# The first MLP product of a hybrid encoder block as seven block products, with the residual normalized ahead of it

## The chip, the cores and the metric

One core of one Trainium2 chip runs the whole block in one launch. The metric is device microseconds of that core; a kernel's number is the median of three runs. TensorE (PE) multiplies, VectorE (DVE), ScalarE (ACT) and GpSimd (POOL) do the elementwise work, and the queues of SyncE (SP), ACT and POOL issue the DMAs.

## The reference, cut to what matters

A prompt of 512 tokens and a sample of 256 tokens pass through one layer with shared weights; 16 meta tokens stand ahead of each. All is float32.

```python
u = _rms(h, norm_mix[l])
proj = u @ w_in[l]                      # latents, rotary key, GLU input, gate logits
...                                     # attention and convolution branches
h = h + (g_a * attn + g_c * conv) @ w_out[l]
u = _rms(h, norm_mlp[l])                                             # mean square over 1024 columns
h = h + jnp.square(jax.nn.relu(u @ w_mlp_in[l])) @ w_mlp_out[l]      # 1024 x 4096, then 4096 x 1024
return _rms(h, norm_final)[:, N_META:]
```

The meta tokens are dropped at the end, so from `w_out` on only 768 tokens are computed.

## The kernel before, in words

Every product of two float32 operands is three matmuls of a rounded part and its remainder: hi*hi, hi*lo and lo*hi. A unit is 512 KB of weights. SP loads it into one of four slots of `raw`; ACT rounds it to `whi` (`hi_unit`, L371); POOL subtracts (`lo_unit`, L376) to get `wlo`; PE multiplies (`products`, L389). Each engine has its own program in order, and counters (semaphores) tie them. The stages follow each other on PE: x is normalized and transposed; latents (units 0 to 7); 16 convolution units; 16 gate units; attention over four pairs of heads; `w_o_attn`, `w_conv_out`, `w_out`; first MLP product; second MLP product.

Start: SP issues the meta tokens, three tiles of x, one weight unit, then (after POOL has cleared `tapsrows`) eight small vector loads and the convolution taps, then the other three tiles of x. ACT squares and roots each tile (`x_rms`, L614), DVE scales it (L994), PE transposes it (L1568). PE transposes the taps (L1581) between the third and the fourth tile.

First MLP product: 32 units, each 128 hidden columns over all 1024 inputs, 48 matmuls (half of 512 tokens and half of 256). The residual h is transposed unnormalized (`h_transpose`, 8 times six transposes); the token scale is spread over partitions with 12 matmuls (`spread_rms`, L1885) and multiplied in on DVE while a unit leaves PSUM (L1380); ACT squares (L943). Beside these units 32 copies on SP and 32 accumulating DMAs on POOL (`sum_copy`, `sum_add`, L1468) write sums of two blocks of `w_mlp_out` to DRAM.

Second MLP product: seven products of block sums in place of eight (`MIX`), 8 units each. For one product the sum is not in DRAM: ACT negates the loaded block in place (L914) and a POOL DMA adds the other block to it (L1555). ACT rounds, DVE subtracts (L1366), hidden blocks are combined and split (L1360, L929, L1370).

## Time and profile before

| what | us |
|---|---|
| median of 3 runs (1288.31 to 1291.43) | 1289.13 |
| profiled execution | 1290.69 |
| its span, first to last instruction | 1289.1 |
| PE busy / DVE / ACT / POOL | 1251.3 / 738.5 / 490.5 / 394.8 |
| mean granted clock of PE | 0.994 |

The profiled execution is 1.6 us longer than its span; what is counted in the trace is the span. PE busy is the union of its matmuls; what a matmul costs is read from the spacing of starts, since their modelled ends overlap.

### The profile page before, as it was taken

How to read it: one execution, taken by the hardware profiler on the slowest of the kernel's cores; microseconds unless marked ns; L12 is line 12 of the kernel's file. 1: busy time of each engine (PE TensorE's matmuls, PEld its weight loads, DVE VectorE, ACT ScalarE, POOL GpSimd, SP SyncE). 2: the span in 40 equal slices, each digit the busy share in tenths (PEclk: the TensorE clock that was granted, in tenths of full speed). 3: DMA queues.
4: the chain of work that ended last, by engine and by line, in shares of the span. 5: the costliest groups of instructions: out<-in, count | busy, mean ns of one | idle time of the engine just before them, and what ended most of it. 6: DMA issues, size and time to landing. Idle time of an engine off the chain costs nothing.

```text
span 1289.1 us, 18449 instructions
## 1 busy us (share of the span) xinstructions
PE 1251.3 (97%) x7037; PEld 1083.4 (84%) x7037; DVE 738.5 (57%) x888; ACT 490.5 (38%) x737; POOL 394.8 (31%) x252
## 2 busy tenths in 40 slices
PE   5999999999999999989999999999999999999997
PEld 4888888888888998878888888888888888887886
DVE  4205999999977877784743123111011136876887
ACT  5234211122256666663522134211222234455455
POOL 1443322233333333326322323344444310020101
PEclk8999999999999999999999999999999999999999
DMA  6222212333220101104344135777777664386443
GB/s 186 69 71 53 76 51 66 90 115 108 87 74 17 35 22 29 49 1 149 109 122 177 66 131 131 181 188 189 187 186 193 137 190 131 131 199 183 125 131 114
DMA packets 145926, 146.55 MB, mean 114 GB/s; under 512 B 11231, under 2 KB 107549, under 8 KB 145868
## 3 DMA queue, kind: packets, MB, share of 16 engines
q1 hardware_dynamic: 132684, 118.48, 29.8%
q0 software_dynamic: 10880, 20.97, 9.4%
q10 hardware_dynamic: 2304, 6.29, 1.2%
q8 instruction: 39, 0.64, 0.2%
q14 instruction: 19, 0.16, 0.0%
HBM read 136.29 MB, written 42.99 MB: 139 GB/s over the span
## 4 chain that ended last, share of the span: by engine, by line
PE 86%; issue 4%; DVE 4%; ACT 2%; POOL 2%; DMA 1%; SPq 0%; POOLq 0%; ACTq 0%; DVEq 0%
PE psum L389 55%; PE psum L1918 17%; PE psum L1839 5%; PE psum L1715 3%; PE psum L1745 2%; POOL wlo L376 1%; PE psum L1680 1%; PE psum L1603 1%; PE psum L1727 1%; DMA xt<-in_x_prompt 1%; DVE ptlo L1166 1%; DVE negmax L1154 1%; DVE olo L1231 1%; PE psum L1846 0%; ACT uhi L623 0%
## 5 line engine op out<-in xcount | busy, mean ns | idle before, releaser
L376 POOL TENSOR_TENSOR wlo<-raw,whi 128x1024 fp32r<-128x1024 f32 (+1 forms) x112 | 258.5, 2308 | 511.4 <-ACT whi L371 511.2
L1074 DVE SCALAR_TENSOR_TENSOR psum<-cs,convw,psum 128x799 f32<-128x799 f32 x196 | 189.4, 1048 | 0.0
L371 ACT ACTIVATE whi<-raw 128x1024 fp32r<-128x1024 f32 (+1 forms) x112 | 112.8, 1007 | 123.4 <-PE psum L389 76.0
L1380 DVE SCALAR_TENSOR_TENSOR hid<-psum,rbc 128x768 f32 (+1 forms) x32 | 30.6, 958 | 218.1 <-PE psum L389 218.0
L389 PE MATMUL psum<-uhi,whi 128*128 128x512 f32 x592 | 152.3, 338 | 0.8 <-POOL wlo L376 0.8
L389 PE MATMUL psum<-uhi,wlo 128*128 128x512 f32 x592 | 152.9, 339 | 0.0
L389 PE MATMUL psum<-ulo,whi 128*128 128x512 f32 x592 | 152.6, 339 | 0.0
L389 PE MATMUL psum<-u2hi,whi 128*128 128x512 f32 (+1 forms) x512 | 130.8, 336 | 0.0
L389 PE MATMUL psum<-u2lo,whi 128*128 128x512 f32 (+1 forms) x512 | 130.3, 335 | 0.0
L389 PE MATMUL psum<-u2hi,wlo 128*128 128x512 f32 (+1 forms) x512 | 130.3, 335 | 0.0
L943 ACT ACTIVATE hid<-hid (+1 forms) x32 | 27.1, 847 | 202.3 <-DVE hid L1380 202.3
L389 PEld LDWEIGHTS psum<-uhi,whi 128*128 128x128 f32 x592 | 91.4, 188 | 14.8 <-POOL wlo L376 1.6
L389 PEld LDWEIGHTS psum<-uhi,wlo 128*128 128x128 f32 x592 | 91.7, 188 | 12.9
L389 PEld LDWEIGHTS psum<-ulo,whi 128*128 128x128 f32 x592 | 91.5, 188 | 12.4
L1918 PE MATMUL psum<-whi,hidhi 128*128 128x512 f32 x228 | 88.9, 390 | 1.2 <-DVE hidlo L1370 1.2
L1918 PE MATMUL psum<-whi,hidlo 128*128 128x512 f32 x228 | 88.7, 389 | 0.0
L1918 PE MATMUL psum<-wlo,hidhi 128*128 128x512 f32 x228 | 88.7, 389 | 0.0
L389 PEld LDWEIGHTS psum<-u2lo,whi 128*128 128x128 f32 x512 | 77.7, 188 | 11.2
L389 PEld LDWEIGHTS psum<-u2hi,wlo 128*128 128x128 f32 x512 | 77.6, 188 | 11.1
L389 PEld LDWEIGHTS psum<-u2hi,whi 128*128 128x128 f32 x512 | 77.6, 188 | 11.0
L1366 DVE TENSOR_TENSOR wlo<-raw,whi 128x1024 fp32r<-128x1024 f32 x38 | 46.5, 1224 | 34.6 <-ACT whi L923 34.6
L923 ACT ACTIVATE whi<-raw 128x1024 fp32r<-128x1024 f32 x38 | 40.2, 1058 | 61.4 <-PE psum L1918 58.0
(243 smaller groups left out, 2455.4 us busy)
## 6 DMA issues: line engine op xcount, KB each, us to landing
raw<-in_w_in SPq DMA_DIRECT2D x38, 512.0 KB, 4.0
raw<-in_w_mlp_in SPq DMA_DIRECT2D x32, 512.0 KB, 4.1
wsums<-in_w_mlp_out SPq DMA_DIRECT2D x32, 512.0 KB, 7.2
wsums<-in_w_mlp_out POOLq DMA_DIRECT2D x32, 512.0 KB, 7.4
raw<-wsums SPq DMA_DIRECT2D x32, 512.0 KB, 3.3
raw<-in_w_mlp_out SPq DMA_DIRECT2D x24, 512.0 KB, 3.7
gates<-gout ACTq DMA_DIRECT2D x16, 384.0 KB, 2.3
gin<-gates SPq DMA_DIRECT2D x16, 384.0 KB, 3.1
```

Of the source, the lines that this page charges most:

```text
L371: nc.scalar.activation(whi[:, c % 2, 0:w], raw[:, c % 4, 0:w], ACT.Copy).then_inc(hi_ready, 1)
L376: gp.tensor_tensor(out=wlo[:, c % 2, 0:w], in0=raw[:, c % 4, 0:w], in1=whi[:, c % 2, 0:w].bitcast(F32), op=ALU.subtract).then_inc(lo_ready, 1)
L389: mm = nc.tensor.matmul(out[:, o0:o0 + n], a, b[:, k, c0:c0 + n], start=first and step == 0, stop=last and step == 2)
L923: nc.scalar.activation(whf[m % 3], raw[:, m % 4], ACT.Copy).then_inc(wmhi_ready, 1)
L943: nc.scalar.activation(r, r, ACT.Square).then_inc(hid_ready, 1)
L1074: ins = nc.vector.scalar_tensor_tensor(out=out, in0=src, scalar=w, in1=a, op0=ALU.mult, op1=ALU.add)
L1366: nc.vector.tensor_tensor(out=wlf[m % 3], in0=raw[:, m % 4], in1=whf[m % 3].bitcast(F32), op=ALU.subtract).then_inc(wmlo_ready, 1)
L1380: nc.vector.scalar_tensor_tensor(out=hid[:, ds(i * 4 + c, 1), :], in0=psum[:, pair:pair + 1, 0:TQ], scalar=0.0, in1=rbc[:, :].rearrange("p ...
L1715: mm = nc.tensor.matmul(psum[:, q % 2, e * HALF:e * HALF + n], a[:, c0:c0 + P], b[:, grp["k0"] + k0:grp["k0"] + k0 + n], start=step == 0, ...
L1745: mm = nc.tensor.matmul(bank[:, 7, 0:2 * P], a[:, vt, hh * VD:(hh + 1) * VD], r[:, blk % 2, e, :], start=e == 0 and step == 0, stop=False)
L1839: mm = nc.tensor.matmul(out, a, b[:, kk, :], start=first and step == 0, stop=last and step == 2)
L1918: mm = nc.tensor.matmul(bank[:, FF_BANKS[p % 2][tt]], a, b[:, kk, :], start=jj == 0 and kk == 0 and step == 0, stop=jj == STEPS - 1 and kk ...
```

## The change

1. The first MLP product is done as seven products of blocks (`IN_MIX`): hidden columns in two halves, tokens in two thirds of 384 each (prompt and sample together are 768), inputs in two halves of 512. A unit is 512 inputs by 256 hidden columns, 24 matmuls of 384 columns; there are 56 units. Blocks of `hid` are first copied from PSUM on ACT with their sign, later contributions are added or subtracted on DVE (`hid_drain`), and after the last one DVE does relu and square in one instruction.
2. The residual is scaled by its token's rms before it is transposed (`h1n`, `h_scale`), so `diag`, `rbc` and `spread_rms` go. 16 groups of three transposes are evicted to `u2raw`; sums of its blocks are made by DVE (`u2_sum`), rounded by ACT and subtracted by DVE.
3. The right half of `w_out` is taken in another order: tiles 0 to 2 of units 2 and 3, tiles 3 to 5 of unit 2, the first four transpose groups, tiles 3 to 5 of unit 3.
4. The sums of `w_mlp_in` blocks (`isums`, 32 copies and 32 accumulating DMAs) are made beside convolution and gates, those of `w_mlp_out` beside attention; nothing of that is left beside the MLP. One product of the first MLP product, like one of the second, is negated on ACT and added by a POOL DMA; in the first MLP product POOL also does the subtractions, in program order with those DMAs.
5. The weights of both MLP products use a ring of six slots (`mraw`, remainder written over the raw block). `MIX` is reordered so that its first product needs blocks finished before the last first-stage product.
6. x is loaded first, five tiles ahead of the first weight unit; the small vectors go by ACT's queue; taps are loaded after three more weight units and transposed after unit 2.

```diff
-SUMS = (((0, 0), (1, 0)), ((1, 0), (1, 1)), ((0, 1), (1, 1)), ((0, 0), (0, 1)))
+SUMS = (((0, 1), (1, 1)), ((0, 0), (1, 0)), ((1, 0), (1, 1)), ((0, 0), (0, 1)))
+IN_SUMS = (((1, 0), (1, 1)), ((0, 0), (0, 1)), ((0, 1), (1, 1)), ((1, 0), (0, 0)))
+IN_MIX = (
+    dict(a=((1, 0), (1, 1)), b=((0, 0),), to=((1, 0, 1), (1, 1, -1))),
+    dict(a=((1, 1),), b=((1, 0), (0, 0)), sign=-1, to=((1, 0, 1), (0, 0, -1))),
+    dict(a=((0, 0), (0, 1)), b=((1, 1),), to=((0, 0, -1), (0, 1, 1))),
+    dict(a=((0, 0),), b=((0, 1), (1, 1)), sign=-1, to=((0, 1, 1), (1, 1, -1))),
+    dict(a=((1, 1), (0, 0)), negate=True, b=((0, 0), (1, 1)), sign=1, to=((0, 0, 1), (1, 1, -1))),
+    dict(a=((0, 1), (1, 1)), b=((1, 0), (1, 1)), sign=1, to=((0, 0, 1),)),
+    dict(a=((1, 0), (0, 0)), b=((0, 0), (0, 1)), sign=1, to=((1, 1, 1),)),
+)
...
 # SP
-            for i in X_ORDER[:4]:
+            for i in X_ORDER[:5]:
                 load_x(i)
             columns(win, 0, 0, 0, slice(0, P))
...
             def conv_units(i):
                 for c in range(4):
...
+                    in_sum_copy(c, i)
...
+                for h in range(2):
+                    for c in range(4):
+                        sum_copy(c, i * 2 + h)
...
+            for x in range(2 * IN_UNITS):
+                if x < 4:
+                    sp.wait_ge(lo_ready, U_OUT + 5 + x)
                 else:
-                    sp.wait_ge(wmlo_ready, m - 3)
+                    sp.wait_ge(unit_used, U_IN + x - RING + 1)
...
+                sp.dma_start(x_place(x), x_block(x, 0)).then_inc(m_landed[x % RING], 16)
 # ACT
+            for name, (r, n) in VEC.items():
+                act.dma_start(vecrows[r:r + n, :], t[name][0].rearrange("(k p) -> k p", p=P)).then_inc(consts_landed, 16)
             act.wait_ge(setup, 5)
...
+            for m in range(IN_UNITS):
+                p, jj = m // STEPS, m % STEPS
+                if m + 2 < IN_UNITS:
+                    x_hi(m + 2)
+                else:
+                    mix_hi(m + 2 - IN_UNITS)
+                for n, (_, _, sign) in enumerate(IN_MIX[p]["to"]):
+                    if in_visits(p, n)[0] == p:
...
+                        nc.scalar.activation(c_block(m, n), c_banks(m), ACT.Copy, scale=float(sign)).then_inc(hid_copied, 1)
+                x_negate(m + 4)
+                if p + 1 < len(IN_MIX) and jj in (3, 4):
+                    u2_hi(p + 1, jj - 3)
 # DVE
+            for m in range(IN_UNITS):
...
+                hid_drain(m)
+                if p + 1 < len(IN_MIX):
+                    if jj in (4, 5):
+                        u2_lo(p + 1, jj - 4)
+                    if jj in (2, 3):
+                        u2_sum(p + 1, jj - 2)
+                if m == IN_UNITS - 4:
+                    mix_hidden(0)
+                if m in (IN_UNITS - 3, IN_UNITS - 2):
+                    mix_lo(m - IN_UNITS + 3)
 # POOL
             def conv_step(i):
                 for c in range(4):
                     lo_unit(gp, U_CONV, i, c + 1)
+                    in_sum_add(c, i)
...
                         gp.tensor_scalar(prob[:, q % 2, 0:n], prob[:, q % 2, 0:n], rsum[:, q % 4:q % 4 + 1], 1.0,
                                          ALU.mult, ALU.mult).then_inc(p_ready, 1)
+                        if 1 <= q < 5:
+                            sum_add(q - 1, p * 2 + hh)
...
+            def x_add(x):
+                if x_negated(x):
+                    gp.wait_ge(wneg_ready, negated_before(x + 1))
+                    gp.dma_start(x_place(x), x_block(x, 1), accum_op=ALU.add).then_inc(wsum_landed[x % 3], 16)
+            for x in range(IN_UNITS):
+                gp.wait_ge(mhi_ready, x + 1)
+                gp.tensor_tensor(out=mlo[x % RING], in0=mraw[x % RING], in1=mhi[x % 3].bitcast(F32),
+                                 op=ALU.subtract).then_inc(inlo_ready, 1)
+                if x + 2 < IN_UNITS:
+                    x_add(x + 2)
 # PE
+            for c in range(2):
+                right_half(c, range(NT), c == 0).then_inc(unit_used, 1)
+            right_half(2, range(TT), False)
+            right_half(3, range(TT), True)
+            right_half(2, range(TT, NT), False).then_inc(unit_used, 1)
+            for n in range(4):
...
+                h_transposes(n)
+            right_half(3, range(TT, NT), True).then_inc(unit_used, 1)
+            for m in range(IN_UNITS):
...
+                pe.wait_ge(inlo_ready, m + 1)
...
+                    wait(pe, hid_copied, in_copies(m - 1))
+                    wait(pe, hid_added, in_adds(m - 1))
...
+                for k in range(KD // 2):
...
+                    if 1 <= m < 4:
+                        h_transposes(4 * m + k)
+                    uh, ul = u2hi[p % 2][:, k, :], u2lo[p % 2][:, k, :]
+                    for e in range(2):
+                        for step, (a, b) in enumerate(((wh, uh), (wh, ul), (wl, uh))):
+                            mm = nc.tensor.matmul(bank[:, 2 * (m % 2) + e, 0:THIRD], a[:, k, e * P:(e + 1) * P], b,
+                                                  start=k == 0 and step == 0, stop=k == KD // 2 - 1 and step == 2)
+                mm.then_inc(unit_used, 1)
```

## Rows read from the trace of the kernel before

**Rows 1.** Windows: length, busy (count) PE, PEld, DVE, ACT, POOL, clock, DMA.
```profile
145.00:368.00 223.00, 223.00 (x1271) 195.66 (x1271) 220.64 (x247) 45.66 (x48) 68.36 (x30) 1.00 0.30 87
368.00:568.00 200.00, 191.05 (x1379) 174.90 (x1378) 148.13 (x242) 132.10 (x286) 73.56 (x78) 1.00 0.11 30
797.00:1051.00 254.00, 254.00 (x1468) 222.13 (x1467) 32.87 (x35) 55.52 (x62) 99.33 (x59) 1.00 0.73 182
1056.00:1281.00 225.00, 224.37 (x987) 185.20 (x988) 176.12 (x192) 112.48 (x142) 19.81 (x14) 1.00 0.51 145
```

**Rows 2.** Chain that ended last; columns: start, duration (us), what ran.
```profile
462.88 1.42 PE psum L1745 x12
795.82 1.34 PE psum L1885 x12
797.15 253.78 PE psum L389 x1464
1050.96 0.97 DVE hid L1380
1056.23 110.46 PE psum L1918 x486
```

**Rows 3.** Timeline of the start: start, duration (us), engine, operation, [idle before].
```profile
3.32 0.63 SPq L483 DMA_DIRECT2D vecrows<-in_norm_mix  x1
5.51 1.06 ACT L614 ACTIVATE junk<-xt 128x1024 f32<-128x1024 f32 x1 [0.94 <-DMA xt<-in_x_prompt]
6.55 0.25 SPq L484 DMA_DIRECT2D tapsrows<-in_conv_w  x1
6.89 1.04 ACT L614 ACTIVATE junk<-xt 128x1024 f32<-128x1024 f32 x1
16.40 1.06 PE L1581 MATMUL psum<-ident,tapsrows 32*128 32x32 f32 x8 [4.53 <-DMA tapsrows<-in_conv_w]
17.63 1.06 ACT L614 ACTIVATE junk<-xt 128x1024 f32<-128x1024 f32 x1 [6.68 <-DMA xt<-in_x_prompt]
20.14 3.25 PE L1568 MATMUL psum<-ident,xt 128*128 128x128 f32 x14 [2.69 <-DVE xt L994]
```

**Rows 4.** Timeline of POOL beside the first MLP product, one unit.
```profile
820.86 2.40 POOL L376 TENSOR_TENSOR wlo<-raw,whi 128x1024 fp32r<-128x1024 f32 x1 [4.91 <-ACT whi L371]
823.21 1.05 POOL L1468 DMA_DIRECT2D wsums<-in_w_mlp_out  x1
```

**Rows 5.** Groups by line, shapes apart: count, busy us, mean ns, idle before.
```profile
L371 ACT ACTIVATE whi<-raw 128x1024 fp32r<-128x1024 f32 x96 | 100.9, 1051 | 122.2 <-PE psum L389 76.0 <-PE psum L1839 37.4 <-ACT gout L707 7.5
L1380 DVE SCALAR_TENSOR_TENSOR hid<-psum,rbc 128x768 f32 x24 | 23.0, 958 | 176.8 <-PE psum L389 176.8
```

**Rows 6.** Accumulating DMAs into SBUF (line 1555): issue to landing, of 8.
```profile
DMA to landing us min/median/max: 6.5/7.3/8.8
```

**Rows 7.** POOL timeline of line 1555, first and last of eight.
```profile
1133.41 1.23 POOL L1555 DMA_DIRECT2D raw<-in_w_mlp_out  x1 [91.75 <-ACT raw L914]
1167.35 1.20 POOL L1555 DMA_DIRECT2D raw<-in_w_mlp_out  x1 [3.64 <-ACT raw L914]
```

**Rows 8.** DMA queues from 1130 to 1180 us: packets, MB, share of 16 engines.
```profile
q0 software_dynamic: 2176, 4.19, 53.6%
q1 hardware_dynamic: 2724, 6.26, 35.5%
```

**Rows 9.** DMA issues of the page: count, KB each, median us to landing.
```profile
raw<-in_w_mlp_in SPq DMA_DIRECT2D x32, 512.0 KB, 4.1
```

**Rows 10.** Timeline of POOL in attention: two neighbouring scalings of the probabilities.
```profile
461.27 0.72 POOL L1503 TENSOR_SCALAR prob<-prob,rsum 128x528 f32<-128x528 f32 x1 [1.27 <-DVE rsum L1160]
462.64 0.49 POOL L1503 TENSOR_SCALAR prob<-prob,rsum 128x272 f32<-128x272 f32 x1 [0.65 <-DVE rsum L1160]
```

**Rows 11.** Timeline of POOL and DVE where two operations overlap.
```profile
96.95 2.40 POOL L376 TENSOR_TENSOR wlo<-raw,whi 128x1024 fp32r<-128x1024 f32 x1
97.08 3.10 DVE L1023 TENSOR_TENSOR krt<-krt,krsw 128x784 f32<-128x784 f32 x1 [1.01 <-POOL krsw L1463]
```

More of the change, by code:

```diff
@@ L422, in sum_squares @@
             mm.then_inc(ss_mm, 1)
[L424 to L432 removed]
+        wm = t["w_mlp_out"][0].rearrange("(u b a p) n -> p u b a n", a=2, b=2, p=P)
@@ L447, in hid_block, with c_banks, u2_block, u2_source @@
+        def c_banks(m):
+            return psum[:, m % 2, :].rearrange("p (b n) -> p b n", b=2)[:, :, 0:THIRD]
+        def u2_block(p, which, part):
+            half, tokens = IN_MIX[p]["b"][which]
+            return u2raw[:, 4 * half + 2 * part:4 * half + 2 * part + 2, tokens * THIRD:(tokens + 1) * THIRD]
+        def u2_source(p, part):
+            if len(IN_MIX[p]["b"]) > 1:
+                return u2sum[p % 2][:, 2 * part:2 * part + 2, :]
+            return u2_block(p, 0, part)
         def hid_block(m, which):
@@ L1351, in _, with h_add @@
-            dve.wait_ge(rbc_mm, 1)
-            nc.vector.tensor_copy(rbc[:, :], psum[:, 2, 0:TQ]).then_inc(rbc_ready, 1)
-            dve.wait_ge(rbc_ready, 1)
+            def h_add(half, i):
+                if half == 0:
+                    tile_made(out_tile, U_OUT + 4, 0, i)
+                elif i < NT - 1:
+                    dve.wait_ge(right_tile, i + 1)
+                else:
+                    dve.wait_ge(unit_used, U_IN)
+                dve.wait_ge(h_landed[0 if i < 4 else 1], 16)
+                hx = h1[:, i, half * HALF:(half + 1) * HALF]
+                nc.vector.tensor_tensor(out=hx, in0=bank[:, (4 + 6 * half + i) % 8], in1=hx, op=ALU.add).then_inc(h_ready, 1)
@@ new lines, in h_scale, with u2_sum @@
+            def h_scale(i):
+                dve.wait_ge(h_root, i + 1)
+                nc.vector.reciprocal(rstd[:, i:i + 1], root[:, i:i + 1]).then_inc(h_rstd, 1)
+                dve.wait_ge(h_rstd, i + 1)
+                dve.wait_ge(h_ready, NT + i + 1)
+                nc.vector.tensor_scalar(h1n[:, i], h1[:, i], rstd[:, i:i + 1], None, ALU.mult).then_inc(h_scaled, 1)
+            def u2_sum(p, part):
+                if len(IN_MIX[p]["b"]) > 1:
+                    dve.wait_ge(u2_act, 4)
+                    dve.wait_ge(u2_dve, 4 if p == 1 else 12)
+                    if p > 1:
+                        dve.wait_ge(unit_used, U_IN + (p - 1) * STEPS)
+                    nc.vector.tensor_tensor(out=u2_source(p, part), in0=u2_block(p, 0, part), in1=u2_block(p, 1, part),
+                                            op=ALU.add if IN_MIX[p]["sign"] > 0 else ALU.subtract).then_inc(usum_ready, 1)
@@ new lines, in u2_lo, with u2_evict @@
+            def u2_lo(p, part):
+                dve.wait_ge(u2hi_ready, 2 * p + part + 1)
+                if p > 1:
+                    dve.wait_ge(unit_used, U_IN + (p - 1) * STEPS)
+                nc.vector.tensor_tensor(out=u2lo[p % 2][:, 2 * part:2 * part + 2, :], in0=u2_source(p, part),
+                                        in1=u2hi[p % 2][:, 2 * part:2 * part + 2, :].bitcast(F32), op=ALU.subtract).then_inc(u2lo_ready, 1)
+            def u2_evict(n):
+                half, k = turned(n)
+                dve.wait_ge(u2t_ready, n + 1)
+                nc.vector.tensor_scalar(u2raw[:, k, half * THIRD:(half + 1) * THIRD], bank[:, turned_bank(n), 0:THIRD],
+                                        vcol("norm_mlp", k), None, ALU.mult).then_inc(u2_dve, 1)
@@ L1900, in _, with right_half @@
-            rolled(pe, KF // 4, in_step, peel=1, last=1)
+            def right_half(c, tiles, by_tile):
+                pe.wait_ge(lo_ready, U_OUT + 4 + c + 1)
+                wh, wl = weights(c % 2, 2, HALF)
+                order = [(kk, tt) for tt in tiles for kk in range(2)] if by_tile else [(kk, tt) for kk in range(2) for tt in tiles]
+                for kk, tt in order:
+                    if c == 0 and kk == 0:
+                        out_bank_free(1, tt)
+                    a_hi, a_lo = z(0, c, kk, tt)
+                    for step, (a, b) in enumerate(((a_hi, wh), (a_hi, wl), (a_lo, wh))):
+                        mm = nc.tensor.matmul(bank[:, (10 + tt) % 8], a, b[:, kk, :], start=c == 0 and kk == 0 and step == 0,
+                                              stop=c == 3 and kk == 1 and step == 2)
+                    if c == 3 and kk == 1 and tt < NT - 1:
+                        mm.then_inc(right_tile, 1)
+                return mm
```

404 lines of the change are left out of this document (210 added, 194 removed).

## The prediction

> **What bounds the kernel now.** I first read busy time by stage. In the convolution and gate stage and beside the first MLP product PE is busy in every microsecond, in the second MLP product for 224.4 of 225, in attention for 191 of 200 [rows 1]: the kernel is a queue of matmuls, and the clock is 1.00 in all four windows. Other engines matter only where they make PE wait. Second I read the chain of waits for what a matmul costs and for the seams: in the first MLP product it stays on PE for 253.78 us and 1464 matmuls, then leaves PE from 1050.96 to 1056.23 us, when the last unit goes through relu, square, rounding and subtraction before the second product can begin [rows 2]. Third the timeline of the start, where PE waits 4.53 us for the taps and 2.69 us for the fourth tile of x [rows 3]. Idle time of DVE, ACT and POOL beside the MLP is what the change spends.
>
> **First MLP product.** Before: 32 units of 48 matmuls, half of 512 and half of 256 columns, 384 on average. The chain gives 253.78/1464 = 0.1734 us per matmul [rows 2], so 8.32 us a unit and 266.3 us in all. After: 56 units of 24 matmuls, all of 384 columns. No row has 384 columns. Below: halfway between 256 columns (1.42/12 = 0.118 us) and 512 (110.46/486 = 0.2273 us) is 0.1728; above: the old mean itself, 0.1734 [rows 2]. I take 0.1734, which is measured on this operand mix: 1344 x 0.1734 = 233.0 us, 4.16 us a unit. **Gain 33.3 us**, at most 34.
>
> **What hides the added work in a unit of 4.16 us.** POOL: a subtraction of 2.40 us [rows 4]. ACT: a rounding of 1.05 us, and at most two copies of 768 elements out of PSUM, which I price like DVE's eviction of the same size, 0.96 us [rows 5]; 3.0 us. DVE: at most two additions and one relu-square of 0.96 us, in some units a block sum or a remainder of the same size, 3.8 us. All fit. A result two units old frees the banks, so a late drain has a whole unit of slack. Weights for a unit are now loaded five units, 21 us, ahead, and landed in 4.1 us before [rows 9]. If that cover goes, each unit costs PE what the longest engine needs over 4.16 us; that happens in one place, below.
>
> **The seams.** The 12 matmuls of `spread_rms` go: 1.34 us [rows 2]. The residual's transposes are 48 before and after. The gap of 1056.23 - 1050.96 = 5.3 us goes [rows 2]: the reordered `MIX` needs blocks finished by the sixth product, and ACT and DVE prepare the first two units during the last three units of the first product. Late next is DVE's third preparation: behind two drains it ends about as PE reaches it; I cost that at nothing, at most 1 us. Ahead of the first unit PE has 18 matmuls of `w_out` (18 x 0.2273 = 4.1 us) while tile 2 is added, squared, rooted and scaled, some 3 us by operations like those of [rows 3, 5]; nothing, at most 1.5 us. **Gain 6.6 us.**
>
> **The start.** The fourth tile of x is squared at 17.63 us because its DMA is issued behind eight vector loads and the taps (3.32 to 6.55 us). Tiles one and two are squared at 5.51 and 6.89, so a fourth that is issued with them comes at 5.51 + 3 x 1.38 = 9.6 [rows 3]. ACT now issues the vector loads itself, 3.2 us of issue at SP's pace; it has a table load and the meta tile to do before 5.51, so I add 1.1 us: 10.7 in place of 17.63, 6.9 us earlier. Upper bound: PE's two waits together, 7.2. The taps' transposes (1.06) leave the start and come back after unit 2, so 1.0 is taken off; lower bound 2, if the fourth tile lands late. **Gain 5.9 us.**
>
> **Sums beside convolution, gates and attention.** POOL issues 32 more DMAs of 1.05 us [rows 4] in the first two stages, where it is busy 68 of 223 us, and the DMA share is 0.30 there; the same sums beside 512 KB loads made 0.73 [rows 1]. The new sums have 1 KB rows in place of 2 KB: the share is between 0.7 and, if a row costs the same whatever its length, just above 1. Loads are issued three units (25 us) ahead, and nothing waits for these sums until the MLP: nothing. SP is moved past 64 copies, each waiting only for the copy before it. In attention POOL's 32 issues stand between scalings of probabilities, for which PE waits. Between the fourth and the fifth scaling POOL is idle 0.65 us [rows 10], less than 1.05, so the fifth comes 0.4 to 0.6 us late; PE has a 1.42 us block ahead of that transpose [rows 2]. I take **1 us lost**, between 0 and 32 x 0.6 = 19.
>
> **The negated product.** Here the change adds a wait. In product 4 ACT negates a block, a POOL DMA adds the other, ACT rounds the sum, POOL subtracts. POOL's program is: subtract x, then issue the addition for x+2. Subtraction x waits for rounding x, which waits for addition x to land. So the addition for x+2, and every subtraction behind it, stands behind the landing for x: a loop of two units of 7.3 us to land [rows 6] + 1.05 to round [rows 5] + 2.40 to subtract [rows 4] + 0.2 between engines = 10.95 us, where PE takes 8.32. Eight units make three full turns: 3 x 2.63 = 7.9 us; the first comes some 0.5 us late, and the added row lengths (1 KB) lengthen the landing a little. I take **9 us lost**. Lower end 4.5: landing 6.5 [rows 6] and 1 us of lead. Upper end 28: landing 8.8, a second issue time of 1.2 [rows 7] and a second engine time, 0.536 x 50/8 = 3.35 us [rows 8], make the loop 17.0, so 3 x 8.7 and a late start. I stay near the median, as the bytes are the same as in that row.
>
> A rule is weighed against this. DVE's sum of two SBUF operands, 784 elements, took 3.10 us and ended 0.8 us after a POOL subtraction that began just before it [rows 11], while DVE's 768 take 0.96 alone [rows 5]. The Trainium skill, "SBUF — State Buffer", its part on the two separate sides of the memory, says that a DVE operation with two SBUF inputs and a GpSimd operation that reads SBUF exclude each other for the whole instruction. The trace agrees in this pair. What it would do here is the first rival below.
>
> **Sum.** 33.3 + 6.6 + 5.9 - 1 - 9 = 35.8 us. From the profiled execution, 1290.69: 1254.9; that execution is 1.6 above the median of the runs, so on their scale 1253.3. I say **1254**, by its own bounds 1243 to 1272.
>
> **Rivals.**
> - *POOL and DVE take turns.* The relu-squares, block sums and remainders have two SBUF operands; with a subtraction they need 2.40 + 2 x 0.96 = 4.3 us of a 4.16 us unit in a few units, which slack takes up, but in product 4 up to three remainders delay subtractions in the loop: 3 x 0.96. **1257**, chance 0.14. For: [rows 11]; against: they collide only if they start so.
> - *The negated product costs nothing.* In the second MLP product the eight additions went out every (1167.35 - 1133.41)/7 = 4.85 us [rows 7], over PE's 4.1 us, and PE was short of work for 0.6 us in the whole stage [rows 1]: lead absorbed it. **1245**, chance 0.17. Against: there no subtraction stood in POOL's queue.
> - *The sums cost where they are made.* The late scalings reach PE each time: 19 us in place of 1. **1272**, chance 0.14. For: attention is the stage where PE already waits 9 of 200 us [rows 1]; against: a block of PE work lies between.
> - *Slower.* In attention four additions are issued within some 8 us. One took 3.35 us of all DMA engines into SBUF [rows 8], so four need 13. Before, they came one in about 8 us or 4.85. If POOL's issue holds the engine until the queue has room, the scalings wait: 5 us and more in each of 8 half pairs. 36/8 = 4.5 us is the point from which the gain is gone; at 6 us, 48 lost: **1302**. Chance 0.05: the issues in the trace took 1.05 and 1.2 us [rows 4, 7], but none came so close together.
> - The remaining 0.02: effects cancel and no change is seen.
>
> **Numbers.** The forecast's own case has 0.48, and with the rivals of 1245 and 1257 it fills 1243 to 1272, which also reaches the third rival's edge. What a measurement of this kernel can tell from no change is about 0.3%, 4 us. Faster 0.93 (the forecast and the first three rivals), same 0.02, slower 0.05.
>
> **What would show it.** First product: 24 matmuls in 4.16 us, starts 0.173 apart. Units 32 to 39: PE waiting for POOL's subtraction, in every second unit by some 2.6 us, ACT's rounding waiting for a DMA. No gap between the products. The fourth tile's transposes near 13 us in place of 20.14 [rows 3]. Attention as long as before within 2 us. Wrong, if PE waits outside product 4 by more than 5 us in sum, if the 384-column matmul starts further than 0.18 apart, or if the convolution stage stretches.

## The result, and the profile after

The changed kernel takes **1259.55 us** (median of 4 runs, 1257.99 to 1263.15), the kernel before, run beside it, 1289.14 (4 runs, 1288.31 to 1291.43): ratio 0.9772, 95% interval 0.9747 to 0.9796. The forecast was 1254 with a range of 1243 to 1272. The profiled execution took 1260.22 us for a span of 1258.6, at a mean granted clock of 0.996.

Where the time went is read from starts of matmuls in both timelines. A line is the same matmul in both; the last column is what the stretch since the line above gained.

| first matmul of | before, us | after, us | gained |
|---|---|---|---|
| the fourth pair of convolution units | 144.76 | 141.67 | 3.1 |
| `w_o_attn` | 573.11 | 570.30 | -0.3 |
| first MLP product | 780.36 | 774.28 | 3.3 |
| second MLP product | 1050.76 | 1020.58 | 24.1 |
| (the last matmul) | 1281.45 | 1250.98 | 0.3 |

In the third line 1.3 us is only moved: 24 transposes of the residual stood in that stretch before, and 12 do after; they are now in the first product. So the first product gained 25.4 and the stretch ahead of it 2.0. The seven block products of the first product are counted from 0: product 3 is units 24 to 31, the negated product 4 units 32 to 39.

Windows by stage of the changed kernel, in the columns of [rows 1] (convolution and gates, attention, first product, second product):

```profile
141.00:365.00 224.00, 223.81 (x1275) 195.94 (x1274) 221.63 (x248) 45.98 (x48) 98.47 (x58) 1.00 0.90 207
365.00:566.00 201.00, 191.77 (x1386) 175.71 (x1385) 148.75 (x244) 132.95 (x288) 108.47 (x111) 1.00 0.82 186
776.00:1020.00 244.00, 237.08 (x1369) 234.22 (x1368) 161.01 (x138) 100.44 (x114) 152.14 (x63) 1.00 0.50 138
1021.00:1251.00 230.00, 228.34 (x1007) 188.40 (x1005) 176.36 (x195) 114.38 (x144) 20.66 (x14) 1.00 0.49 144
```

Against [rows 1], PE is as busy in the first two stages as before, although the DMA share there went from 0.30 and 0.11 to 0.90 and 0.82 (the sums) and POOL is busy for 30 and 35 us more. In the first product PE, which never waited, now idles for 6.9 us; DVE went from 33 to 161 us busy.

The chain that ended last, from the first product on (columns of [rows 2]):

```profile
794.23 88.42 PE psum L2095 x510
...
898.91 3.16 DVE u2sum L1474
...
902.09 0.02 ACT u2hi L1024
...
902.84 1.05 ACT whi L1007
...
903.98 3.01 POOL rawlo L1725
906.98 6.19 DMA raw<-in_w_mlp_in
...
947.31 2.39 POOL rawlo L1725
949.75 70.99 PE psum L2095 x408
1020.74 130.62 PE psum L2116 x576
1151.38 8.70 DMA raw<-in_w_mlp_out
```

A matmul of 384 columns takes 88.42/510 = 0.1734 us. The chain leaves PE at 882.65 us already. Up to 902 it runs over DVE's additions, relu-squares and block sums of product 3. The block sum at 898.91 releases a rounding on ACT (902.09); behind that, in ACT's program, stands the rounding of the next weights (902.84), behind that POOL's subtraction and the second addition (906.98). From there to 950 us the chain goes round POOL's subtraction and the landing of an addition: the loop of the negated product. From issue to issue its turns of two units take 9.7, 9.7 and 12.5 us (906.98, 916.69, 926.35, 938.84). The DMA share from 904 to 944 is 1.00, so how much of a landing is queueing for DMA engines stays open. Between the two products the chain stays on PE. It leaves it once more at 1151.38, for an addition in the second product's negated part.

The timeline of PE, only the rows where it waited in the first product (a last one at 949.75 waited 0.97 us for POOL), and then the POOL and DVE timelines at the end of product 3:

```profile
903.93 0.41 PE L2095 MATMUL psum<-u2hi,whx 128*128 128x384 f32 x1 [0.49 <-DVE hid L1509]
...
909.73 0.41 PE L2095 MATMUL psum<-u2hi,whi 128*128 128x384 f32 x1 [1.36 <-DVE hid L1509]
...
914.88 0.41 PE L2095 MATMUL psum<-u2hi,whi 128*128 128x384 f32 x1 [0.72 <-DVE hid L1509]
...
933.03 0.44 PE L2095 MATMUL psum<-u2hi,whx 128*128 128x384 f32 x1 [0.85 <-POOL rawlo L1725]
...
938.93 0.45 PE L2095 MATMUL psum<-u2hi,whi 128*128 128x384 f32 x1 [1.44 <-POOL rawlo L1725]
...
944.31 0.44 PE L2095 MATMUL psum<-u2hi,whi 128*128 128x384 f32 x1 [0.94 <-POOL rawlo L1725]
```

```profile
898.17 3.07 POOL L1725 TENSOR_TENSOR rawlo<-raw,whx 128x1024 fp32r<-128x1024 f32 x1 [3.59 <-ACT whx L1007]
901.18 1.34 POOL L1721 DMA_DIRECT2D raw<-in_w_mlp_in  x1
...
938.84 1.28 POOL L1721 DMA_DIRECT2D raw<-in_w_mlp_in  x1
```

```profile
898.03 0.96 DVE L1515 SCALAR_TENSOR_TENSOR hid<-hid 128x768 f32<-128x768 f32 x1
898.91 3.15 DVE L1474 TENSOR_TENSOR u2sum<-u2raw 128x768 f32<-128x768 f32 x1
901.98 1.81 DVE L1509 TENSOR_TENSOR hid<-hid,psum 128x768 f32<-128x768 f32 x2
```

Two different engines keep PE waiting: DVE in product 3 (the wait at 914.88, ahead of product 4's first unit, is for product 3's last additions), POOL in the last four units of product 4. The eight additions go out (938.84 - 901.18)/7 = 5.38 us apart. DVE's block sum (L1474) takes 3.15 us beside the subtraction that runs from 898.17 to 901.24, and ends 0.8 after its end; on its own, at 895.32, the same line takes 0.94. The addition out of PSUM (L1509, two in 1.81) is not lengthened. Additions land about as [rows 6] led to expect (all sixteen of both products; the eight of the first take 6.1 to 9.0):

```profile
DMA to landing us min/median/max: 6.0/7.5/10.5
```

The timeline of the start, against [rows 3]:

```profile
10.96 1.04 ACT L708 ACTIVATE junk<-xt 128x1024 f32<-128x1024 f32 x1
...
13.45 2.34 POOL L425 TENSOR_TENSOR wlo<-raw,whi 128x1024 fp32r<-128x1024 f32 x1 [9.95 <-ACT whi L420]
...
13.88 0.22 DVE L1123 COPY vec<-psum 128x62 f32<-128x62 f32 x1 [1.84 <-PE psum L1760]
...
14.20 2.13 DVE L1114 TENSOR_SCALAR xt<-xt,rstd 128x1024 f32<-128x1024 f32 x1
...
16.39 2.71 PE L1750 MATMUL psum<-ident,xt 128*128 128x128 f32 x14 [2.56 <-DVE xt L1114]
```

The fourth tile is squared at 10.96 in place of 17.63. But its scaling stands in DVE's program behind the copy of the vectors, and then takes 2.13 us beside a POOL subtraction (the other tiles' took 0.75), so its transposes come at 16.39 in place of 20.14.

### The profile page after: what moved, and what is told of

It reads as the page before. It is cut to its first block, busy times and chain, and to the rows that moved or that the text cites. A ratio compares the mean times of both kernels' runs of the same rounds, so it can differ in the third digit from the quotient of the medians.

```text
span 1258.6 us, 18355 instructions
## 1 busy us (share of the span) xinstructions
PE 1217.3 (97%) x6833; PEld 1081.8 (86%) x6833; DVE 860.9 (68%) x984; ACT 528.9 (42%) x785; POOL 512.6 (41%) x316
## 4 chain that ended last, share of the span: by engine, by line
PE 78%; issue 7%; DMA 4%; POOL 3%; DVE 3%; ACT 3%; SPq 0%; ACTq 0%; POOLq 0%; DVEq 0%
PE psum L438 34%; PE psum L2116 17%; PE psum L2095 14%; PE psum L2024 3%; PE psum L2062 3%; PE psum L1900 2%; DMA raw<-in_w_mlp_in 2%; PE psum L1930 2%; POOL wlo L425 1%; PE psum L1781 1%; DMA wsums<-in_w_mlp_out 1%; POOL rawlo L1725 1%; PE psum L1912 1%; DMA raw<-in_w_mlp_out 1%; PE psum L1750 1%
## 5 line engine op out<-in xcount | busy, mean ns | idle before, releaser
L425 POOL TENSOR_TENSOR wlo<-raw,whi 128x1024 fp32r<-128x1024 f32 (+1 forms) x80 | 181.9, 2274 | 302.6 <-ACT whi L420 299.4
L1509 DVE TENSOR_TENSOR hid<-hid,psum 128x768 f32<-128x768 f32 x64 | 59.4, 949 | 70.8 <-PE psum L2095 38.4
L2095 PE MATMUL psum<-u2hi,whi 128*128 128x384 f32 x296 | 100.0, 338 | 4.5 <-POOL rawlo L1725 2.4
L438 PEld LDWEIGHTS psum<-ulo,whi 128*128 128x128 f32 x592 | 91.5, 188 | 12.5
L2095 PE MATMUL psum<-u2hi,rawlo 128*128 128x384 f32 x304 | 101.7, 335 | 0.0
L2095 PE MATMUL psum<-u2lo,whi 128*128 128x384 f32 x296 | 98.9, 334 | 0.0
L2116 PE MATMUL psum<-rawlo,hidhi 128*128 128x512 f32 x228 | 88.7, 389 | 0.0
L1007 ACT ACTIVATE whx<-raw 128x1024 fp32r<-128x1024 f32 x38 | 40.2, 1058 | 62.7 <-PE psum L2116 27.7
L1725 POOL TENSOR_TENSOR rawlo<-raw,whi 128x1024 fp32r<-128x1024 f32 x19 | 49.6, 2609 | 39.4 <-ACT whi L1007 39.4
L1725 POOL TENSOR_TENSOR rawlo<-raw,whx 128x1024 fp32r<-128x1024 f32 x19 | 50.5, 2660 | 30.9 <-ACT whx L1007 30.9
L1007 ACT ACTIVATE whi<-rawx 128x1024 fp32r<-128x1024 f32 x36 | 38.1, 1057 | 51.3 <-PE psum L2116 25.7
```

The lines of the kernel that those rows point to most:

```text
L425: gp.tensor_tensor(out=wlo[:, c % 2, 0:w], in0=raw[:, c % 4, 0:w], in1=whi[:, c % 2, 0:w].bitcast(F32), op=ALU.subtract).then_inc(lo_ready, 1)
L438: mm = nc.tensor.matmul(out[:, o0:o0 + n], a, b[:, k, c0:c0 + n], start=first and step == 0, stop=last and step == 2)
L1007: nc.scalar.activation(mhi[x % 3], mraw[x % RING], ACT.Copy).then_inc(mhi_ready, 1)
L1509: nc.vector.tensor_tensor(out=block_, in0=block_, in1=c_banks(m), op=ALU.add if sign > 0 else ALU.subtract).then_inc(hid_added, 1)
L1725: gp.tensor_tensor(out=mlo[x % RING], in0=mraw[x % RING], in1=mhi[x % 3].bitcast(F32), op=ALU.subtract).then_inc(inlo_ready, 1)
L2095: mm = nc.tensor.matmul(bank[:, 2 * (m % 2) + e, 0:THIRD], a[:, k, e * P:(e + 1) * P], b, start=k == 0 and step == 0, stop=k == KD // 2 - ...
```

## The experiments

Three theories of the 9.4 us that the first product loses (246.3 us from its first matmul to the second product's, less 233.0 of matmuls and 36 x 0.109 of transposes). **Theory 1**: the loop of product 4 (round, subtract, issue, land) sets it. **Theory 2**: the DMA engines do. **Theory 3**: DVE and POOL take turns. All kernels were timed in 5 rounds against the kernel before. "Product" is the length from the first matmul of the first product to the first of the second, read from each timeline; it leaves out what happens earlier, which scatters by 2 us (last section). It scatters itself: in the five profiles whose edits leave the work of the first product alone (the changed kernel, after_again, scale_first, no_sums, seam_late) it is 245.3 to 247.1, so a difference of less than about 2 us shows nothing. "PE idle" is 70 less PE's busy time from 880 to 950 us.

| kernel | median us (lowest to highest) | ratio, interval | product | PE idle |
|---|---|---|---|---|
| after_again | 1259.78 (1258.88 to 1262.31) | 0.9772 [0.9759, 0.9785] | 246.1 | 6.7 |
| three_ahead | 1261.50 (1253.99 to 1262.50) | 0.9765 [0.9741, 0.9789] | 245.2 | 5.5 |
| late_relu | 1266.03 (1264.64 to 1268.90) | 0.9820 [0.9806, 0.9833] | 251.2 | 4.8 |
| scale_first | 1258.75 (1258.08 to 1262.43) | 0.9764 [0.9751, 0.9777] | 247.1 | 6.9 |
| relu_on_act | 1261.61 (1260.42 to 1262.63) | 0.9780 [0.9767, 0.9793] | 245.7 | 5.2 |
| relu_on_act_three | 1252.02 (1249.95 to 1255.24) | 0.9713 [0.9694, 0.9732] | 240.6 | 2.8 |
| no_addition | 1257.43 (1256.56 to 1258.57) | 0.9749 [0.9735, 0.9762] | 241.9 | 3.8 |
| no_sums | 1260.74 (1258.94 to 1263.71) | 0.9777 [0.9761, 0.9794] | 245.3 | 6.1 |
| zero_remainders | 1258.22 (1256.19 to 1261.59) | 0.9761 [0.9746, 0.9776] | 241.2 | 2.8 |
| seam_late | 1262.76 (1260.77 to 1264.97) | 0.9785 [0.9771, 0.9798] | 245.6 | 6.8 |
| start_alone (edit of before) | 1287.84 (1285.52 to 1289.35) | 0.9980 [0.9971, 0.9989] | | |
| all_four | 1259.38 (1258.67 to 1262.41) | 0.9766 [0.9753, 0.9779] | 238.9 | 1.4 |

**after_again**, the base of the first group, unedited.

> The changed kernel, nothing edited: the base that the other kernels of this group are compared with. All theories: 1259.5 us, within 1.5, and the kernel before at 1289.

As expected.

**three_ahead**, the loop over three units in place of two:

```diff
-                x_negate(m + 4)
+                x_negate(m + 5)
...
-                if x + 2 < IN_UNITS:
-                    x_add(x + 2)
+                if x + 3 < IN_UNITS:
+                    x_add(x + 3)
```

> ACT negates a block one unit earlier (five units ahead in place of four) and POOL issues the addition for unit x+3, not x+2, behind the subtraction of unit x. Theory 1, the loop 'landing, rounding, subtraction, next issue' over two units sets the 5.38 us of a unit in product 4: the loop now spans three units, 10.95/3 = 3.65 us a unit, below PE's 4.16, so PE's four waits for POOL's subtraction (4.2 us by the profile, about 5 with the ends of the matmuls modelled) go: 1254.5 us, and the additions go out about 4.2 us apart. Theory 2, the DMA engines are the limit (3.35 us for an addition and 1.65 for a load make 5.0 us a unit): the additions still go out about 5.0 us apart, landing takes longer than 7.5 us, ACT's wait for it stays: 1258 to 1260 us. Theory 3, POOL and DVE take turns: POOL's waits go in part, the three waits for DVE at the end of product 3 (2.6 us) stay under each theory.

None of the three forecasts came. The two longest of PE's four waits in the product (the others are 0.51 and 0.55, for DVE too), the window in which the clock fell (columns of [rows 1]), and one of the additions on POOL:

```profile
910.90 0.41 PE L2095 MATMUL psum<-u2hi,whi 128*128 128x384 f32 x1 [1.39 <-DVE hid L1509]
...
918.33 0.41 PE L2095 MATMUL psum<-u2hi,whi 128*128 128x384 f32 x1 [3.01 <-DVE hid L1509]
```

```profile
920.00:924.00 4.00, 4.00 (x17) 4.00 (x16) 2.76 (x2) 1.06 (x1) 3.25 (x2) 0.62 0.96 131
```

```profile
931.37 1.29 POOL L1721 DMA_DIRECT2D raw<-in_w_mlp_in  x1 [3.41 <-ACT raw L998]
```

All waits for POOL are gone, as theory 1 says. But the additions came no closer, (934.56 - 897.19)/7 = 5.34 us apart, where theory 1 had 4.2 and theory 2 5.0. Two of them wait on POOL for ACT's negation (2.75 us at 918.27, 3.41 at 931.37), and ACT waited for the plain load under it. That load could go out only when PE had freed its slot: the one behind 931.37 went out at 924.35, after PE's long wait. So this run does not show that the loop alone set the pace before. POOL's work also comes closer together at the end of product 3 (subtractions from 905.15, 908.98 and 912.41), and DVE, which takes turns with it, is later (a remainder at 912.60 takes 3.75): the waits for DVE grew from 2.6 to 5.5 us. After the longest one the granted clock averaged 0.62 over 4 us, that is, part of them at the lower of the clock's two levels (1.00 is 2.4 GHz, 0.50 is 1.2 GHz): 17 matmuls, where the next windows of 4 us, at 1.00, show 25. One of the five runs took 1253.99; no trace shows what it did otherwise.

**late_relu**, product 3's relu-squares moved to product 5:

```diff
-                for n in range(len(IN_MIX[p]["to"])):
-                    if in_visits(p, n)[-1] == p:
-                        block_ = c_block(m, n)
+                done = [c_block(m, n) for n in range(len(IN_MIX[p]["to"])) if in_visits(p, n)[-1] == p and p != 3]
+                if p == 5:
+                    done.append(c_block(m - 2 * STEPS, 0))
+                for block_ in done:
...
```

> The relu-squares of the block finished by product 3 (eight of 768 elements, two SBUF operands) are made in product 5 in place of product 3. Theory 3, DVE is late at the end of product 3 because its operations with two SBUF operands take turns with POOL's subtractions (2.4 to 3.2 us each in place of 0.96), and these waits add to the time: the three waits go, 1256.5 us. Theory 1 or 2, the additions of product 4 free-run from the first issue near 901 us, and PE only arrives earlier in front of them: the three waits for DVE go, the waits for POOL in product 4 grow by as much, 1259.5 us, within 0.7.

PE's timeline, three of its five waits in the product (0.51 and 1.36 for DVE stand ahead of the last):

```profile
922.96 0.69 PE L2097 MATMUL psum<-u2hi,whi 128*128 128x384 f32 x1 [2.50 <-POOL wlo L1727]
...
939.53 0.44 PE L2097 MATMUL psum<-u2hi,whi 128*128 128x384 f32 x1 [2.33 <-POOL rawlo L1727]
...
992.24 0.41 PE L2097 MATMUL psum<-u2hi,whx 128*128 128x384 f32 x1 [2.69 <-DVE hid L1509]
```

Product 3's waits for DVE went. In product 4 the waits for POOL became fewer and longer, 4.8 us in place of the base's 4.4, and the mean granted clock of 908 to 950 us was 0.92 in place of 1.00: PE came earlier to additions that had kept their pace, as theory 1 said, and some of what had been won went in clock. What no theory had: the eight relu-squares now make product 5 late, in the pattern of product 3 (4.6 us for DVE). The kernel is 6 us slower than the base.

**scale_first**, DVE's program at the start:

```diff
-            x_scale(0), x_scale(1), x_scale(2), x_scale(3)
+            x_scale(0), x_scale(1), x_scale(2), x_scale(3), x_scale(4)
             dve.wait_ge(vec_t, 1)
             nc.vector.tensor_copy(vec[:, :], bank[:, 6, 0:NVEC]).then_inc(vec_ready, 1)
-            x_scale(4)
```

> DVE scales the fourth tile of x before it copies the vectors out of PSUM, not behind. Theory A, the fourth tile's scaling (14.20 us, and 2.13 long beside a POOL subtraction) is what PE waits for: the scaling runs near 11.7 for 0.75 us, its transposes directly behind that of the vectors near 13.7 in place of 16.39, first matmul near 16.4 in place of 18.76, and 2.3 us of it last to the end: 1257.2 us. Theory B, something else is late next (the rounding of the first weights at 12.33 and its POOL subtraction to 15.8, or loads of the next units): the first matmul moves by under 1 us, or PE waits later in the first 60 us: above 1258.5 us.

Timeline of the start:

```profile
12.71 0.75 DVE L1114 TENSOR_SCALAR xt<-xt,rstd 128x1024 f32<-128x1024 f32 x1
...
13.91 2.22 PE L1749 MATMUL psum<-ident,xt 128*128 128x128 f32 x14
...
16.18 0.47 PE L1780 MATMUL psum<-uhi,whi 128*128 128x512 f32 x1
```

Theory A in the trace: the scaling takes 0.75 and the first matmul is at 16.18 in place of 18.76. At the first matmul of `w_o_attn` the kernel is still 2.5 us ahead of the base (the two later kernels with this edit, relu_on_act_three and all_four, 1.6 and 1.5). In the time only 1.0 is seen, less than the runs scatter: in this execution the stretch up to the first product took 2.3 us longer and the product, whose work this edit leaves alone, 1.0 longer: PE waited 3.28 us for POOL at 940.11.

**relu_on_act**, product 3's relu-squares by ACT, in no later product:

```diff
+                if 3 * STEPS <= m - 2 < 4 * STEPS:
+                    block_ = c_block(m - 2, 0)
+                    act.wait_ge(hid_added, in_adds(m - 1))
+                    nc.scalar.activation(block_, block_, ACT.Relu).then_inc(hid_relu, 1)
+                    act.wait_ge(hid_relu, m - 1 - 3 * STEPS)
+                    nc.scalar.activation(block_, block_, ACT.Square).then_inc(hid_whole, 1)
```

> The eight relu-squares that end product 3 are made by ACT (a relu and a square of 768 elements, two units after DVE's addition), not by DVE: nothing is moved into a later product. Theory 1, product 4's additions free-run from the first issue near 901 us, 5.3 us apart, so PE that comes earlier only waits longer there: DVE's three waits at the end of product 3 (2.3 to 2.6 us) go, POOL's in product 4 grow by as much, 1259.8 us, within 1. Theory 3, the waits for DVE are a loss of their own: 1257 us. In the kernel with the relu in product 5 both happened and product 5's waits for DVE (4.6 us) came on top; here product 5 has none.

1261.61, and PE waits for DVE nowhere in the product. Three waits for POOL of 2.54, 1.60 and 1.09 us, 5.2 together, stand where the base has 4.4 in five, and the mean clock from 908 to 950 us is 0.96. The product is 0.4 us shorter than the base's, which is within its scatter: theory 1's side, though the time lies 0.8 us above its range.

**relu_on_act_three**, the three edits above together (three_ahead, scale_first, relu_on_act).

> Three edits together: ACT makes product 3's relu-squares, negation and additions run one unit earlier, and the fourth tile of x is scaled before the vectors are copied. If both waits are what is lost in the first product (DVE beside POOL at the end of product 3, and the loop of additions in product 4), and each edit alone only moved the loss to the other, then together PE waits under 2 us in the whole product and its clock stays at 1.00 there: 1251 us, within 2. If DMA throughput sets product 4 (additions 5.3 us apart with every edit so far), PE still waits for POOL at the end of product 4, 3 us or more: 1255 to 1258 us.

**1252.02 us**, the best of all kernels. The window of 908 to 950 us and the waits of PE in the product:

```profile
908.00:950.00 42.00, 39.23 (x225) 38.39 (x224) 27.49 (x22) 22.49 (x25) 30.78 (x16) 1.00 0.84 194
```

```profile
919.42 0.45 PE L2101 MATMUL psum<-u2hi,whi 128*128 128x384 f32 x1 [1.36 <-POOL wlo L1731]
...
933.77 0.41 PE L2101 MATMUL psum<-u2hi,whi 128*128 128x384 f32 x1 [1.41 <-DVE hid L1515]
```

Each edit alone had moved the loss to the other engine; together they remove 5.5 of the 9.4 us. The forecast's 1251, within 2, came, with 2.8 us of waiting in place of under 2. The additions now go out 4.74 us apart (894.02 to 927.17), still over PE's 4.16, and the DMA share is 0.95 to 1.15 in each 4 us from 900 to 936: with the loop widened, full DMA engines (theory 2) are the likely pace, argued from this share and not tested. The first addition goes out earlier (894 in place of 901), and PE waits for POOL only once.

**no_addition**: product 4 reads a plain block (no negation, no addition).

```diff
-    return (IN_MIX[x // STEPS] if x < IN_UNITS else MIX[x // STEPS - len(IN_MIX)]).get("negate", False)
+    return x >= IN_UNITS and MIX[x // STEPS - len(IN_MIX)].get("negate", False)
```

> Left out: the negation and the addition in product 4 of the first MLP product, whose weights are then one plain block (its result is another). This is the upper bound of what the negated product costs. Theory 1: POOL's waits in product 4 (4.4 us) and the part of DVE's at the end of product 3 that the issues of additions bring about go: 1252 to 1254 us, with up to 2.5 us of DVE's waits left, as the subtractions of POOL stay. Theory 3, taking turns alone makes most of the loss: above 1256 us.

1257.43, on theory 3's side: without the loop PE still waits, for DVE, 3.7 us (0.49, 1.36 and 1.83). Leaving the addition out, alone, takes 246.1 - 241.9 = 4.2 us off the product.

**no_sums**: all 64 sums, their copies and the waits for them left out, plain blocks loaded in their place.

```diff
-                    in_sum_copy(c, i)
...
-                        if 1 <= q < 5:
-                            sum_add(q - 1, p * 2 + hh)
...
```

> Left out: all 64 sums of weight blocks beside convolution, gates and attention (copies, additions and the waits on them); the products read a plain block of the weights in place of each sum (rows of 512 bytes or 2 KB in place of whole sums). The forecast had 1 us for them, all in attention: 1259 us, attention shorter by 0.5 to 1. Rival, the sums cost more than the waits show (DMA share 0.9 beside convolution and gates): 1255 us or less, convolution and gates shorter too.

Windows of the two stages, to be held against those of the changed kernel above:

```profile
141.00:365.00 224.00, 223.81 (x1275) 195.88 (x1273) 221.63 (x248) 46.00 (x48) 69.02 (x31) 1.00 0.30 87
365.00:566.00 201.00, 191.85 (x1388) 175.87 (x1387) 148.75 (x244) 133.25 (x289) 74.62 (x79) 1.00 0.11 30
```

PE's busy time is the same in both stages with DMA shares of 0.30 and 0.11 in place of 0.90 and 0.82: the sums are hidden. `w_o_attn` starts 0.3 us earlier, a little less than forecast, and the time is the base's.

**zero_remainders**: POOL writes zeros for units 26 to 33, in place of subtracting.

```diff
+                if 26 <= x < 34:
+                    gp.memset(mlo[x % RING].bitcast(F32), 0.0).then_inc(inlo_ready, 1)
+                else:
...
```

> Left out: for units 26 to 33 of the first MLP product POOL fills the remainder of the weights with zeros in place of subtracting (its instruction reads no SBUF; the result is another). POOL makes these units while PE is in product 3. Taking turns: DVE's relu-squares and block sums at the end of product 3 take 0.95 us each, none over 1.3, where they took 2.1 to 3.2 beside subtractions, and its three waits (2.3 to 2.6 us) go. Rival, DVE is late there by its own work or by POOL's issues of additions: its instructions stay at 2 to 3 us and the waits stay. For the time: the additions go out earlier by up to 2 us, as POOL is free sooner, and then keep their 5.3 us: 1257 to 1260 us.

DVE's timeline at the end of product 3:

```profile
898.81 0.96 DVE L1515 SCALAR_TENSOR_TENSOR hid<-hid 128x768 f32<-128x768 f32 x1
899.69 0.95 DVE L1474 TENSOR_TENSOR u2sum<-u2raw 128x768 f32<-128x768 f32 x1
```

Every relu-square, block sum and remainder there takes 0.95 or 0.96, and the waits for DVE are gone, with the same DVE program: it was the subtractions that made DVE late, not its own work. Additions stayed 5.3 us apart, but the first went out 123.5 us after the product's first matmul (899.56), against 126.9 (901.18) in the changed kernel, 1.6 us of this because ACT waited less for DVE's block sums, the rest because a write of zeros takes 0.96 where that subtraction took 3.07. So the 4.9 us by which the product is shorter are not DVE's waits alone. PE still waits 2.8 us for POOL in product 4. The profile is of the fastest of the five runs; the median is 1.6 below the base's.

**seam_late**: the second unit of the second product is prepared only when the hidden layer is whole, as in the kernel before.

```diff
-                else:
-                    mix_hi(m + 2 - IN_UNITS)
+                elif m + 2 == IN_UNITS:
+                    mix_hi(0)
...
+            act.wait_ge(hid_whole, 4 * STEPS)
+            for m in range(1, FF_UNITS):
...
```

> The second unit of the second MLP product is prepared (rounding on ACT, subtractions and block difference on DVE) only when the hidden layer is whole, as in the kernel before; the first unit is prepared early as there. The forecast counted 5.3 us for the gap that this had left in the chain of waits: if PE had waited so long, 1264 to 1265 us. Rival, from PE's own rows of before (PE was at work on the first unit in that stretch and waited 1.21 us for DVE's remainder): 1.2 us, 1261 us, PE's wait ahead of the second unit between 0.8 and 2.

The second unit's first matmul:

```profile
1028.38 0.47 PE L2120 MATMUL psum<-whx,hidhi 128*128 128x512 f32 x1 [2.17 <-DVE hidlo L1538]
```

PE waited 2.17 us ahead of it, for DVE's remainder, a little over the rival's bound and far from 5.3; the second product is 1.7 to 2.5 us longer than in the two profiles of the changed kernel.

**start_alone**: the kernel before, with the diff's edits to the loads of x, the vectors and the taps, and nothing else.

> The kernel before with the new start alone: five tiles of x loaded first, the vectors by ACT's queue, the taps later. From the traces of before and after (first matmul of the convolution stage at 144.76 and 141.67): 3.1 us, 1287 us. The forecast's 5.9 us: 1284 us. If the start's gain is lost again further on: 1290 us.

1287.84 against 1290.34 of the kernel before beside it: 2.5 us, between 1.4 and 3.7 by the interval; in its trace the fourth pair of convolution units starts at 143.18, 1.6 us earlier than before. 5.9 is excluded.

**all_four**: as relu_on_act_three, and the same lead in the second product.

```diff
-                x_negate(IN_UNITS + m + 3)
+                x_negate(IN_UNITS + m + 4)
...
-        wsum_landed = [sem(f"wsum_landed{c}") for c in range(3)]
+        wsum_landed = [sem(f"wsum_landed{c}") for c in range(4)]
...
```

> ACT makes product 3's relu-squares, negation and additions one unit earlier in the first MLP product, fourth tile scaled first, and in the second MLP product too the negation runs one unit earlier (a fourth semaphore for the additions). Without the last edit 1252.0 us, with a wait of 1.2 us for DVE in the second product's negated part. If that wait comes from the lead of the additions: it goes, 1251 us. If DMA throughput sets that part (share 1.07): the wait stays, 1252 us.

Neither: 1259.38. The first product is the shortest of all, 238.9 us, but the second is 6 us longer. ACT's first negation there:

```profile
1128.63 1.06 ACT L999 ACTIVATE rawx<-rawx 128x1024 f32<-128x1024 f32 x1 [7.38 <-DMA rawx<-in_w_mlp_out]
```

The negation asks for a load that SP issued at 1123.47, and ACT waits 7.38 us at the head of its queue. Behind it stands the rounding of the next unit's weights, which began at 1129.60 here and at 1123.35 in relu_on_act_three. PE then waits five times, up to 2.18 us, four times for DVE's remainder.

## Why the forecast was right, and where it was off

The forecast's sum was 35.8 us and the profiles show 30.5 (1290.69 to 1260.22): 5.3 less. The largest term was right, the largest loss right in size and in part in place. Two terms were too large, by 7.8 us together; 2.7 us elsewhere made up for part of that, and 2.0 of these are luck. Step by step:

- **First product, +33.3**: right. 1344 matmuls of 384 columns at 0.1734 us, 233.0 us, are what was forecast.
- **The negated product, -9**: the size was right, the place in part. The product loses 9.4 us, with additions 5.38 us apart where the loop was to give 10.95/2 = 5.5; PE waits ahead of each of the last four units, 0.85 to 1.44 us, and not 2.6 in every second one. But only 4.2 go when the addition is left out (no_addition), and 4.9 when DVE no longer takes turns with POOL in product 3 (zero_remainders, which starts the loop earlier too). The forecast's loop and its first rival both happened, and the price of 9 came out because the rival's share, which the term did not hold, filled what the loop did not cost: that the size was met is in part luck. That the loop alone sets the 5.38 us is not shown: with it widened the additions stayed 5.34 apart (three_ahead), and in the changed kernel the DMA share beside it is 1.00. Edits that remove one kind of wait and keep the work win little, because PE runs into the next late engine: three_ahead, late_relu and relu_on_act won at most 1 us of product.
- **Rival "POOL and DVE take turns"**: it happens, and not in product 4 as its sentence had it but ahead of it, in product 3, where each unit asks DVE for two additions and a relu-square, and four of them for a block sum or remainder as well. The forecast let DVE's 3.8 us fit into a unit at 0.96 an operation; beside subtractions the relu-squares took 2.4 to 2.9. Line L1474 took 3.15 us beside a subtraction, 0.94 alone, and 0.95 throughout once POOL wrote without reading. The Trainium skill, "SBUF — State Buffer", "Who interferes with whom", says that a DVE instruction with two SBUF inputs contends with a GpSimd instruction that reads SBUF and not with one that only writes it. The traces agree on both halves.
- **The seams, +6.6**: this is the step that failed. The 12 matmuls of `spread_rms` went (1.34). The gap of 5.3 us was not there: the chain of waits left PE at 1050.96, and I took the whole stretch up to its return for waiting. PE's own rows in the timeline of the kernel before say otherwise (the first two rows are the first and the last matmul of the second product's first unit, the third is the second unit's first):

```profile
1050.76 0.39 PE L1918 MATMUL psum<-whi,hidhi 128*128 128x512 f32 x1
...
1054.64 0.39 PE L1918 MATMUL psum<-whi,hidlo 128*128 128x512 f32 x1
1056.23 0.47 PE L1918 MATMUL psum<-whi,hidhi 128*128 128x512 f32 x1 [1.21 <-DVE hidlo L1370]
```

PE did the first unit of the second product in that stretch and waited 1.21 us. [rows 1] had a sign of it: the 225 us from 1056 to 1281 hold 990 matmuls at 0.2273, and the product has 56 units of 18, 1008, so one unit had run before 1056. No row ahead of the prediction covers PE from 1051 to 1056. seam_late shows a wait of that kind, 2.17 us, and not 5.3. After the change the chain stays on PE across the seam, but 1.66 us of waiting appears at 1165.25 in the second product's negated part, so that product as a whole gained 0.3. In after_again that wait is 0.64 and the gain 1.0.
- **The start, +5.9**: 3.1. The tile is squared when I said (10.96, forecast 10.7); I had followed it through ACT and not through DVE, where its scaling waits behind a copy that waits for PE, and then takes 2.13 us beside POOL. scale_first and the two kernels that keep its edit show that this was worth 1.5 to 2.5 us up to `w_o_attn`; start_alone that what is left is 2.5 (1.4 to 3.7), measured alone.
- **The sums, -1**: -0.3 in attention, nothing in the stage before, as no_sums shows. The rivals "the sums cost where they are made" and "slower" are excluded: POOL's issues between scalings went out without holding it up, at DMA shares of 0.8 to 0.9.
- **Rival "the negated product costs nothing"**: excluded, by the 4.2 us of product that no_addition wins.
- **Not forecast, +2.0**: the stretch from `w_o_attn` to the first product. The edits explain none of it: in scale_first, relu_on_act, no_addition, no_sums and zero_remainders, where they stand too, the stretch took 205.9, which is the 207.25 of before less the 1.3 that moved (last section). The forecast was nearer by these 2 us by luck.

Measured: 25.4 + 0.3 + 3.1 - 0.3 + 2.0 = 30.5. Against the forecast, the seam is 5 us short and the start 2.8, attention and the unforeseen stretch 2.7 better.

## What to carry to other kernels

A row of the chain of waits that is not on PE does not say that PE waits: ask the window or PE's timeline for the same stretch before a gap is put into a sum. When two engines run close behind PE, removing one's delay alone can show nothing or less than nothing; here three_ahead and relu_on_act, worth under 1 us of product each, took 5.5 off it together, and with the start's edit the kernel went from 0.9772 to 0.9713 of the kernel before, 7.6 us. Moving a wait to the head of an in-order queue earlier helps only while its load is already there: the same one-unit lead was part of that gain in the first product, and cost 6 us in the second.

## What the runs showed of the hardware

**Waits cost clock, sometimes.** After the wait of 3.01 us in three_ahead the granted clock of the next 4 us was 0.62; in late_relu a window behind a wait of 2.50 showed 0.60, in relu_on_act one behind 2.54 showed 0.78. In scale_first one of 3.28 was followed by 0.58. But a wait of 2.61 us in seam_late and one of 2.69 in late_relu (at 992.24) were followed by 1.00, while late_relu's 2.33 was followed by 0.57: the length of the wait alone does not decide. In the profile of the changed kernel, whose waits in the product are 1.44 at most, the product's windows stay at 1.00.

**One SBUF operand was held up too.** At the start of the changed kernel DVE's scaling of a tile, 0.75 us for the first three, took 2.13 (14.20 to 16.33) beside a POOL subtraction from 13.45 to 15.79; its only tensor operand in SBUF is the tile.

**The same matmuls ran at two paces at a granted clock of 1.00.** In `w_o_attn`, near 605 us, three pairs of matmuls, each of one with 512 and one with 256 columns, take 1.06 us in the profile of before (starts at 604.65 and 605.71) and 1.04 in that of after (605.07 and 606.11). It is no property of a kernel: from `w_o_attn` to the first product after_again, three_ahead, late_relu and scale_first, in which nothing of that stretch is edited, took 203.6, 205.3, 204.2 and 205.9 us. What decides between the paces stays open. At up to 2.3 us in this stretch alone it may be a good part of the 3 to 4 us by which runs of one kernel differ.
